# Forty-eight modulation tiles formed by VectorE in the first feed-forward stage instead of TensorE in the input stage

## The reference

```python
s_lat = jax.nn.silu(c)
s_ctx = jax.nn.silu(c_ctx)
for i in range(DEPTH):
    m_lat = jnp.split((s_lat @ ada_w[i] + ada_b[i])[:, None, :], 6, axis=-1)
    m_ctx = jnp.split(s_ctx @ ada_w[i] + ada_b[i], 6, axis=-1)
    h_lat = modulate(rmsnorm(x_lat, norm1_g[i]), m_lat[0], m_lat[1])
    h_ctx = modulate(rmsnorm(x_ctx, norm1_g[i]), m_ctx[0], m_ctx[1])
    ...
    x_lat = x_lat + m_lat[2] * y_lat
    x_lat = x_lat + m_lat[5] * swiglu(modulate(rmsnorm(x_lat, norm2_g[i]), m_lat[3], m_lat[4]),
                                      ffn_w_in[i], ffn_w_out[i])
```

## Time and profile before

| | us |
|---|---|
| median of three runs (lowest, highest) | 3424.08 (3423.61, 3424.87) |
| the profiled execution | 3424.37 |
| its span, first to last instruction | 3422.6 |
| PE busy in it | 3212.4 (94%) |
| DVE busy in it | 1672.9 (49%) |
| mean granted clock of TensorE | 0.968 |
| first stage, steps of PE | 63.3 to 471.2 |
| first feed-forward stage | about 1254 to 2182 |

### The profile page before, as it was taken

One profiled execution on the slowest core, in us unless ns is written; L12 is line 12 of the kernel. 1 busy time (PEld: TensorE's weight loads), 2 busy tenths in 40 slices (PEclk: granted clock), 3 DMA queues, 4 the chain that ended last, 5 costly groups with the idle time before them and its releaser, 6 DMA issues. The chain is left out here.

```text
span 3422.6 us, 40199 instructions
## 1 busy us (share of the span) xinstructions
PE 3212.4 (94%) x16098; PEld 2558.8 (75%) x16098; DVE 1672.9 (49%) x2146; ACT 940.4 (27%) x1205; POOL 350.8 (10%) x263
## 2 busy tenths in 40 slices
PE   7999998899866899999999999999969999999999
PEld 6788865455455788888888888778757888888887
DVE  5443237576687452344444444767774433333333
ACT  4222223344311221111111111377773311111111
POOL 1000000477422210000000000200001000000000
PEclk8999999799978999999999999999989999999999
DMA  5666610000311301111111111111103111111111
GB/s 196 228 220 206 203 47 1 0 1 1 134 74 61 117 31 44 37 37 37 37 37 40 40 37 43 71 40 37 40 21 117 59 47 49 49 49 49 43 55 74
DMA packets 65197, 231.67 MB, mean 68 GB/s; under 512 B 7911, under 2 KB 17511, under 8 KB 63560
## 3 DMA queue, kind: packets, MB, share of 16 engines
q1 hardware_dynamic: 50600, 199.26, 16.9%
q0 software_dynamic: 4000, 17.37, 1.4%
q10 hardware_dynamic: 10496, 13.63, 1.2%
HBM read 204.55 MB, written 25.69 MB: 67 GB/s over the span
## 5 line engine op out<-in xcount | busy, mean ns | idle before, releaser
L252 PE MATMUL bank<-h_pair,w_hi 128*128 128x512 f32 (+1 forms) x2448 | 620.0, 380 | 8.1 <-DVE h_pair L1867 7.2
L252 PEld LDWEIGHTS bank<-h_pair,w_hi 128*128 128x128 f32 x2448 | 442.4, 188 | 97.1 <-issue 8.9
L238 DVE TENSOR_TENSOR w_lo<-w_raw,w_hi 128x1024 fp32r<-128x1024 f32 x194 | 264.0, 1361 | 421.1 <-ACT w_hi L232 417.7
L268 PE MATMUL bank<-h_pair,w_hi 128*128 128x512 f32 x1344 | 366.8, 394 | 0.0
L252 PE MATMUL bank<-h_pair,w_lo 128*128 128x512 f32 (+1 forms) x1224 | 353.4, 379 | 0.0
L1798 DVE SCALAR_TENSOR_TENSOR x<-bank,c_mods,x 128x1024 f32<-128x1024 f32 (+3 forms) x280 | 273.9, 1007 | 144.2 <-PE bank L252 141.0
L232 ACT ACTIVATE w_hi<-w_raw 128x1024 fp32r<-128x1024 f32 x194 | 203.7, 1050 | 448.9 <-PE bank L268 218.3
L268 PEld LDWEIGHTS bank<-h_pair,w_hi 128*128 128x128 f32 x1344 | 227.9, 188 | 43.4
L252 PEld LDWEIGHTS bank<-h_pair,w_lo 128*128 128x128 f32 x1224 | 221.2, 188 | 44.1
L268 PE MATMUL bank<-h_pair,w_lo 128*128 128x512 f32 x672 | 208.3, 391 | 0.0
L276 DVE COPY ffn_part<-bank 128x256 f32<-128x256 f32 x42 | 17.8, 425 | 383.4 <-PE bank L268 383.4
(11 more groups left out here) (338 smaller groups left out, 5169.7 us busy)
## 6 DMA issues: line engine op xcount, KB each, us to landing
w_raw<-in_weights SPq DMA_DIRECT2D x194, 512.0 KB, 3.3
ada_late_w<-in_ada_w SPq DMA_DIRECT2D x80, 512.0 KB, 3.7
x<-in_x SPq DMA_DIRECT2D x2, 5120.0 KB, 14.9
h_gate<-u_scratch SPq DMA_DIRECT2D x4, 2560.0 KB, 9.4
ada_w<-in_ada_w SPq DMA_DIRECT2D x16, 512.0 KB, 17.1
u_scratch<-uc POOLq DMA_DIRECT2D x12, 640.0 KB, 5.2
spec_lat<-f_spec ACTq DMA_DIRECT2D x4, 1792.0 KB, 9.2
h_spec<-spec_lat SPq DMA_DIRECT2D x2, 3584.0 KB, 12.4
```

Of the source, the lines that this page charges most:

```text
L238: e.tensor_tensor(k.w_lo[s][:, :], k.w[s][:, :], k.w_hi[s][:, :].bitcast(F32), ALU.subtract).then_inc(k.split_lo[s], 1)
L252: mm = e.matmul(out[:, c:c + m], w[:, c1:c1 + P], x[:, c:c + m], start=(first and kk == 0 and n == 0), stop=(last and kk == kt - 1 and n = ...
L268: mm = e.matmul(out[:, c:c + m], w, x[:, half, c:c + m], start=(first and n == 0), stop=(last and n == 2))
```

## The change

The 48 modulation tiles of the second layer are no longer formed by PE in the first stage. `ADA_TILES` falls from 96 to 48, the list places two tiles in each of items 2 to 17 instead of six in each of items 2 to 14 and two in item 15, and `coefficients` there covers norm 1 alone. In the first feed-forward stage DVE forms them from the weights laid out by rows: `ada_rows` holds for each tile two pieces of [128 outputs, 512 inputs], 96 pieces of 256 KB. PE spreads silu(c) over all partitions into banks 6 and 7 (`spread_c`), and a row product multiplies a piece by the bank and keeps the sum along the row in one column of `late`. Per hidden tile of groups 1 to 8 DVE does six of them, in groups 9 and 10 eight, these for silu(c_ctx), for which PE spreads anew ahead of group 9. After the last one, `late_columns` adds the halves and biases and forms the coefficients of norms 2 and 3. The pieces come through three buffers, two in the room of `ss` and one of its own, loaded by POOL, each when DVE has used what was in it; `ss` is therefore cleared after the last. The hardware loop covers groups 0 to 7 now, four turns; groups 8 and 9 are written out.

```diff
--- before.py
+++ after.py
@@ -85,12 +85,14 @@
...
+LATE, BOTH = 48, 16
+ROWS_LOOPS, ROWS_IN, ROWS_END, ROW_BUFS = 4, 6, 8, 3
...
@@ -426,7 +428,7 @@
 
 
 
-ADA_TILES = 2 * 48
+ADA_TILES = 2 * 48 - LATE
 ADA_FIRST = 2 * KT
 ADA_BUFS = 3
 
@@ -506,7 +508,7 @@
         e.activation(k.mods[:, 2 * n:2 * n + 2], self.turned(k, n), ACT.Copy).then_inc(self.stored, 1)
 
     def coefficients(self, k, e, steps, norms):
...
+
+    def late_columns(self, k, e, steps):
+
+
+        mods = k.mods[:, :].rearrange("p (m w) -> p m w", w=2)[:, ADA_TILES:]
+        halves = k.c["late"][:, :].rearrange("p (m h) -> p m h", h=2)
+        for who, first, count in ((0, 0, LATE), (1, LATE, BOTH)):
+            part = mods[:, 0:count, who]
+            steps(e.tensor_tensor(part, halves[:, first:first + count, 0], halves[:, first:first + count, 1], ALU.add))
+            steps(e.tensor_tensor(part, part, k.ada_b[:, ADA_TILES:ADA_TILES + count], ALU.add))
+        for n, who, at in ((2, 0, 0), (2, 1, 0), (3, 0, 24)):
+            a, b = (k.coef[:, (n * 2 + who) * 16 + 8 * i:(n * 2 + who) * 16 + 8 * i + 8] for i in range(2))
+            steps(e.scalar_tensor_tensor(out=a, in0=mods[:, at + 8:at + 16, who], scalar=1.0,
+                                         in1=k.gains[:, n * KT:(n + 1) * KT], op0=ALU.add, op1=ALU.mult))
+            steps(e.tensor_copy(b, mods[:, at:at + 8, who]))
...
@@ -794,7 +811,7 @@
 
 
 FILTER_PASSES = [(order, half) for order in range(2) for half in range(2)]
-ADA_STEPS = (0, 1, 3, 4, 6, 7)
+ADA_STEPS = (0, 4)
 
 
 def even_in_events(items, tiles, spectra):
...
+    late = [k.at(f"ada_rows{n}", SS0 + n * (D // 2), [P, D // 2]) for n in range(2)] + [k.c["rows"]]
...
+    loops = ROWS_LOOPS if both else end_groups // 2
+    ops = 2 * (LATE + BOTH)
...
     def schedule(e, take_in, take_out):
 
         take_in(0, 0, (w0, a0), True)
-        with e.Fori(0, end // 2) as b:
+        def two(first):
             for n in range(2):
-                g = b * 2 + n
+                g = first + n
                 take_in(g + 1, (n + 1) % 2, in_at(g + 1))
                 take_out(g, n, out_at(g), False)
+
+        with e.Fori(0, loops) as b:
+            two(b * 2)
+        for g in range(2 * loops, end, 2):
+            two(g)
         take_out(end, 0, end_at, True)
...
@@ -1929,7 +1960,21 @@
         def _(e):
             norm.tensor(k, e)
 
+            def spread_c(who):
+                for kk in range(KT):
+                    at = 32 * kk + who
+                    mm = e.matmul(k.bank[:, 6 + kk // 4, kk % 4 * P:(kk % 4 + 1) * P],
+                                  k.silu_c[:, at:at + 1].to_broadcast([P, P]), k.ident[:, :], start=True, stop=True)
+                mm.then_inc(c_rows, 1)
+
+            if both:
+                e.wait_ge(k.rr_ready, norm.bcs + len(norm.chunks))
+                spread_c(0)
+
             def take_in(g, buf, at, first=False):
+                if both and isinstance(g, int) and g == 2 * loops + 1:
+                    e.wait_ge(late_used, 2 * LATE)
+                    spread_c(1)
                 for t in range(HG):
...
+            def row_sums(turn, count, column):
+
+                for j in range(count):
+                    e.wait_ge(late_landed[j % ROW_BUFS], turn * 16 + (j // ROW_BUFS * 16 + 16))
+                    row = late[j % ROW_BUFS]
+                    e.scalar_tensor_tensor(out=row[:, :], in0=row[:, :], scalar=1.0, in1=k.bank[:, 6 + j % 2, :], op0=ALU.mult,
+                                           op1=ALU.mult, accum_out=k.c["late"][:, bass.ds(column + j, 1)]).then_inc(late_used, 1)
+
             def take_in(g, buf, at, first=False):
                 for t in range(HG):
                     if not (first and t == 0):
                         split_lo(k, e, 1, at[0] + t)
+                    if both and first and t == 0:
+                        e.wait_ge(c_rows, 1)
+                    if both and not first:
+                        slot = g * 2 + (t - 2)
+                        if isinstance(g, int):
+                            e.wait_ge(c_rows, 2)
+                            end_rows(slot - 4 * loops)
+                        else:
+                            row_sums(slot * (ROWS_IN // ROW_BUFS), ROWS_IN, slot * ROWS_IN)
...
@@ -2064,6 +2137,16 @@
             @block.gpsimd
             def _(e):
                 e.wait_ge(k.stat_full, norm.n + 1)
+                for n in range(ROW_BUFS):
+                    e.dma_start(late[n][:, :], d["ada_rows"][n]).then_inc(late_landed[n], 16)
+                with e.Fori(0, 2 * LATE // ROW_BUFS - 1) as i:
+                    for n in range(ROW_BUFS):
+                        e.wait_ge(late_used, i * ROW_BUFS + (n + 1))
+                        e.dma_start(late[n][:, :], d["ada_rows"][i * ROW_BUFS + (n + ROW_BUFS)]).then_inc(late_landed[n], 16)
+                for j in range(2 * LATE, ops):
+                    e.wait_ge(late_used, j - ROW_BUFS + 1)
+                    e.dma_start(late[j % ROW_BUFS][:, :], d["ada_rows"][j - 2 * LATE]).then_inc(late_landed[j % ROW_BUFS], 16)
+                e.wait_ge(late_used, ops)
                 sum_squares(k, e, cleared, base, sq, tokens)
...
+    aw = a["ada_w"].reshape(2, KT, P, 48, P)
+    o["ada_w"] = np.ascontiguousarray(np.ascontiguousarray(aw.transpose(0, 3, 2, 1, 4)).reshape(96, P, KT, P)[:ADA_TILES])
+    rows = a["ada_w"][1].T.reshape(48, P, 2, D // 2)[48 - LATE:]
+    o["ada_rows"] = np.ascontiguousarray(rows.transpose(0, 2, 1, 3)).reshape(2 * LATE, P, D // 2)
...
```

More of the change, by code:

```diff
@@ L92 @@
                     ("g_lat", 5), ("rg_w", 40), ("rg_b", 10), ("rg_ba", 40), ("rg_lam", 20), ("rg_sp", 80),
-                    ("stat", 16), ("rstd", 16)):
+                    ("stat", 16), ("rstd", 16), ("late", 2 * (LATE + BOTH)), ("rows", D // 2)):
     CONSTS[_name] = (_at, _len)
@@ L508, in coefficients @@
     def coefficients(self, k, e, steps, norms):
-        first, last = 24 * norms[0], 24 * norms[-1] + (16 if len(norms) == 1 else 24)
+        first, last = 24 * norms[0], 16 if norms == [0] else ADA_TILES
         mods = k.mods[:, :].rearrange("p (m w) -> p m w", w=2)
@@ L1889, in ffn @@
     tokens = T if layer == 0 else LAT
+    end_groups = GROUPS - 1
     norm = Norm(k, 2 * layer + 1)
@@ L1899, in ffn @@
     hid_ready, hi_done, lo_done = (k.sem(f"{n}{layer}") for n in ("ffn_hid", "ffn_hid_hi", "ffn_hid_lo"))
[L1900 to L1901 removed]
+    if both:
+        gate_joined, up_joined, out_joined = (k.sem(f"ffn_{n}_joined") for n in ("gate", "up", "out"))
+        gate_copied, up_copied = (k.sem(f"ffn_{n}_copied") for n in ("gate", "up"))
     part = k.at("ffn_part", R0 + 4 * HG * T + 2 * T, [P, CTX])
@@ L1906, in ffn @@
     half = KT // 2
+    late = [k.at(f"ada_rows{n}", SS0 + n * (D // 2), [P, D // 2]) for n in range(2)] + [k.c["rows"]]
+    if both:
+        late_landed = [k.sem(f"ada_rows_landed{n}") for n in range(ROW_BUFS)]
+        late_used, c_rows, late_steps = k.sem("ada_rows_used"), k.sem("ada_c_rows"), k.sem("ada_late_steps")
+    loops = ROWS_LOOPS if both else end_groups // 2
+    ops = 2 * (LATE + BOTH)
+    assert 4 * ROWS_IN * ROWS_LOOPS == 2 * LATE and 2 * ROWS_END * (end_groups - 2 * ROWS_LOOPS) == 2 * BOTH
     in_at = lambda g: (g * 3 + (w0 - 1), g * 6 + (a0 - 4))
     out_at = lambda g: (g * 3 + (w0 + 4), g * 6 + (a0 + 4))
-    end = GROUPS - 1
+    end = end_groups
     end_at = (w0 + 3 * end + 2, a0 + 6 * end + 2)
```

16 lines of the change are left out of this document (11 added, 5 removed).

## The result

| | before | changed |
|---|---|---|
| median, us | 3423.85 (4 runs, 3421.70 to 3424.87) | 3403.15 (4 runs, 3401.66 to 3404.29) |
| the profiled execution, its span | 3424.37, 3422.6 | 3404.29, 3402.6 |

The account below looks back on a forecast made before the run. PE was taken as the bound, busy 94% of the span. 3424.4 - 32.0 (tiles less those turned into waiting) + 8.0 (clock) + 1.8 + 2.1 (spreads) = 3404.3 us; own range 3396 to 3408, stretched to 3392 to 3414.

Parts of the forecast that it names:

- 48 tiles off PE: First stage: 80 late modulation tiles become 32, each costing PE 0.89 us, so 42.7 us of PE work goes.
- waits for the first spectra: First stage, four filter passes: 12 removed tiles turn into PE waiting for DVE, each wait growing from 0.57 to 3.24 us.
- clock in the first stage: Behind the four grown waits the clock falls at most of them, about 2 us each: 8 us lost, bounds 0 to 11.6.
- first spread: Feed-forward opening: eight broadcast products delay the first weights' products, 1.8 us lost, bounds 0 (DVE's low halves set pace) and 2.1.
- second spread: Ahead of group 9's first tile in the feed-forward stage: the context row's spread has no cover, 2.1 us lost.
- rows, coefficients, other queues: Feed-forward row slots on DVE (7.2, 11.6, last 13.7 us) fit 16.6 us of room; other queues cost nothing: 0 us.
- stretches without a change: Rest of the kernel, outside the two stages touched: no term in the sum, 0 us.
- The rival that put all four falls at 2.9: First stage: clock falls behind all four waits at 2.9 us each, 11.6 us lost, 3407.9 us in all; chance 0.15.
- Rival (3): Feed-forward stage: last four row slots somewhat too long, reload time R near 8.7 us, 10 us more, 3414 us; chance 0.05.
- (4): Feed-forward stage: three buffers too few for eight rows; gain gone at R = 9.9, 3449 us at R = 13; chance 0.05.

Follow-up runs that it names:

- the series with 0, 1, 2 and 4 tiles: Changed kernel (1) with modulation tiles moved so 0, 2 or 4 stand between last filter tile and first spectrum: 3406.55, 3403.15 (1), 3397.70, 3386.89 us.
- the kernel with the shorter first fall: Changed kernel with three spare products instead of ten in front of the first spread at the feed-forward opening: 3404.20 us.
- two row buffers: Changed kernel with two buffers for the rows instead of three: 3402.18 us.
- four tiles: Changed kernel with modulation tiles moved so four instead of one stand before each pass's first spectrum, 32 tiles as before: 3386.89 us.

## Why the prediction was right, step by step

| step | forecast | measured |
|---|---|---|
| 48 tiles off PE | -42.7 | -41.0 (48 x 0.854) |
| waits for the first spectra | +10.7 | +10.6 (12.8 - 2.2) |
| clock in the first stage | +8.0 | +7.6 (2.88 + 3 x 1.56) |
| first spread | +1.8 | +0.2, and 0.6 of clock at the opening |
| second spread | +2.1 | +1.8 |
| rows, coefficients, other queues | 0 | 0 |
| stretches without a change | 0 | +0.4 (+2.2, -2.7, +0.8) |
| in all, of the span | -20.1 | -20.0 |

(The fourth fall's price has no next first spectrum to be read from; it is taken as the second's, since its half clock lasts as long. The spreads and the 0.6 amount to 2.6, of which C to D, 2.45 longer, shows all but 0.15.)

**The tiles and the waits.** The main argument, that a quarter of the removed work stood in front of DVE's chain and only turns into waiting, is exact: 3.24 us forecast, 3.21 measured, and the series with 0, 1, 2 and 4 tiles shows it from both sides. The tile's 0.89 was read at a place where it stands alone, and is 4% too much beside filter tiles and spectra.

**The clock.** That half clock follows these waits was right, and filling the wait showed it. A mean of 2 us for four falls was forecast, and 1.9 came. What lay behind it was less sound: I reasoned from the length of a wait, 2.76 us without a fall against 3.34 with one. The clock fell at all 20 waits of 3.2 us in the first stages of five kernels, at 2.3 in five of eight, and at 2.77 in none of thirteen profiles. Length is one condition and not the rule. The rival that put all four falls at 2.9 had their number right and the price of one alone. The rule of the Trainium skill, TensorE: Matmul & The Clock Gate, HAM oscillation, held in kind, as each of the four waits cost anew; the price ran from 1.6 to 2.9. Taking these four for long waits in its sense was the prediction's own reading.

**The spreads.** Both were sized by a row of eight products in 2.06 us; here they take 1.71. The first one's cover was mis-sized: the 0 was to hold if the halves of h set the pace, and I took 1.8 because PE waited for them only once, for 0.23 us. They do set it: the weights' first products start 0.68 us later with the spread than without, and the first output block 0.2.

**The rows.** 0 was right, with room to spare: 7.4 to 8.0 us for six rows and 10.6 to 11.7 for eight (7.2 and 11.6 forecast), the last 12.9 with its coefficients (13.7), R 4.8 in the slot shown and 5.0 as the median over the slots (4.4), in a room of 16.4 (16.6). Rival (3) needed an R near 8.7, and (4) one of 9.9 to lose the gain. Even two buffers would have done.

**Luck.** The first stage gave 1.2 us less than its 24.0, the feed-forward stage cost 1.45 less than its 3.9. That the total is off by 1 us owes something to the two having opposite signs, and to the untouched stretches adding up to so little. The mean of 1.9 us for a fall is luck too: no single fall cost that, and with the same first stage the kernel with the shorter first fall lost 1.7 us less.

**Those stretches.** Over all thirteen profiles of the same code there, B to C took 777.6 to 783.7 us, and A came at 96.1 to 98.8. Half clock goes with a part of this. Before A it adds up to 30.7, 34.1 or 37.6 us, and A comes at 96.1 to 97.7 with the first and at 98.0 to 98.8 with the other two. From B to C it adds up to 133 to 140 us in the four profiles with the times from 780.1 to 783.7, but in the other nine to 129.8 to 129.9, and these still spread from 777.6 to 779.8. Behind D its sum, 43.0 to 48.1 us, doesn't sort the times. So why stretches without a change move by up to 6 us stays in part open; no run here was made for it.

## What to carry to other kernels

Before counting the work that a change takes off an engine, find for each piece what it stood in front of: the tiles that PE did while DVE's chain ran were free, and moving twelve of the remaining tiles there (3386.89 us) gained 16 us more, where removing 48 tiles had gained 21. Of the 18 us by which A to B got shorter, about 11 are waiting filled with work, and about 8 are the clock, which no longer fell. When you remove work from an engine whose clock follows its activity, look at the wait that is left, and fill it with work that has to be done anyway. For gains below 5 us compare the stretch that the change touches, cut at instructions that both kernels share, since here stretches without a change moved by as much on their own.

## What the runs showed of the hardware

- Waits of 2.3 us let TensorE's clock fall to its lower level in five cases of eight, with the same work around them, and not behind the same ones in two executions. Behind waits of 3.2 to 4.1 us it fell in all 24 cases of the first stage, but the wait of 3.27 us at the end of the feed-forward stage (two row buffers) had no fall behind it, where the wait of 3.32 us above (four tiles) has 16 instructions in 6.07 us at 0.53:

```profile
2145.91:2149.18 3.27, 0.00 (x1) 1.00 0.00 0
2149.18:2155.25 6.07, 6.07 (x28) 1.00 0.00 0
```

- In the first stage a fall costs 1.3 to 1.6 us where half clock lasts 3.41 us and 2.5 to 2.9 where it lasts 6.83. The same program had either at the same wait.
- Twelve or thirteen 128x128 products that compute nothing, in the wait, kept the clock at 1.00 behind it each time, in five waits.
- A DVE product of 128x512 with a running sum takes 0.69 us and lets the next one start 0.61 us after it; reading the sum out is a record of 0.08 us inside that.
